# Expert rows of x loaded as 128 pieces of 768 words, and sorted by ScalarE: one layer of a hybrid decoder with a mixture of experts

## The reference

```python
h = rms_norm(x, norm2_g) * (1 + sc2) + sh2          # (T, D)
g_idx   = top-1 of softmax(h @ w_rg + b_rg)         # 4 groups
e_idx   = top-2 of softmax((h @ w_re + b_re) in that group)   # 8 experts each
weights = g_top * e_top / sum(e_top)
for each expert e, over the tokens xs that chose it:
    gate, up = split(xs @ w_e_in[e], 2)             # w_e_in[e]: (1024, 1024)
    y = (silu(gate) * up) @ w_e_out[e]              # w_e_out[e]: (512, 1024)
x = x + gt2 * (sum over both experts of weights * y)
```

## Time and profile before

| | us |
|---|---|
| median of 3 runs | 1781.41 (1779.94 to 1782.64) |
| profiled execution, first to last instruction (span) | 1778.4 |
| median less span | 3.0 |
| TensorE busy | 1670.4 (94%) |
| VectorE busy | 1012.6 (57%) |
| ScalarE busy | 442.4 (25%) |
| DMA traffic | 363.70 MB, mean 205 GB/s |
| chain that ended last | PE 80%, DMA 14%, DVE 3% |

### The profile page before, as it was taken

One profiled execution on the slowest core, in us unless ns is written; L12 is line 12 of the kernel. 1 busy time (PEld: TensorE's weight loads), 2 busy tenths in 40 slices (PEclk: granted clock), 3 DMA queues, 4 the chain that ended last, 5 costly groups with the idle time before them and its releaser, 6 DMA issues.

```text
span 1778.4 us, 35422 instructions
## 1 busy us (share of the span) xinstructions
PE 1670.4 (94%) x14793; PEld 930.9 (52%) x14793; DVE 1012.6 (57%) x2453; ACT 442.4 (25%) x1072; POOL 211.8 (12%) x311
## 2 busy tenths in 40 slices
PE   5999999999999999999999999987999999999990
PEld 3455444544444545555455545545777775555550
DVE  2486526555555354443544435555778877776754
ACT  5120324333444212222122121112222122122110
POOL 3030000000110222202222051010000000000003
PEclk9999999999999999999999999988999999999995
DMA  9377218001211110101101176489899999999997
GB/s 350 120 265 252 71 71 263 25 24 32 63 48 52 47 33 16 33 21 31 34 16 33 56 292 232 148 284 370 330 425 427 426 427 426 429 427 427 429 422 303
DMA packets 109014, 363.70 MB, mean 205 GB/s; under 512 B 12890, under 2 KB 56840, under 8 KB 96428
## 3 DMA queue, kind: packets, MB, share of 16 engines
q1 hardware_dynamic: 86256, 282.70, 41.0%
q10 hardware_dynamic: 15708, 54.73, 8.4%
q0 software_dynamic: 6960, 25.04, 3.8%
HBM read 316.42 MB, written 58.74 MB: 211 GB/s over the span
## 4 chain that ended last, share of the span: by engine, by line
PE 80%; DMA 14%; DVE 3%; POOL 1%; issue 1%; ACT 1%; SPq 1%; ACTq 0%; POOLq 0%; DVEq 0%
PE bank L298 78%; DMA arena<-in_w_e_out 11%; DMA arena<-in_w_in 1%; POOL arena L759 1%; PE bank L945 1%; DMA arena<-y_slots,ints 1%; SPq L380 1%; DVE arena L2396 0%; DVE arena L1887 0%; PE bank L1233 0%; ACTq L1397 0%; DMA arena<-in_kn_g_c 0%; DVE arena L2386 0%; ACT arena L1523 0%; DMA x_slots<-arena,ints 0%
## 5 line engine op out<-in xcount | busy, mean ns | idle before, releaser
L298 PE MATMUL bank<-arena 128*32 128x256 f32 (+7 forms) x14414 | 1627.4, 388 | 36.4 <-DMA arena<-in_w_e_in 7.1
L298 PEld LDWEIGHTS bank<-arena 128*32 128x32 f32 (+3 forms) x14414 | 884.7, 131 | 748.5 <-issue 548.1
L2386 DVE STREAM_TRANSPOSE arena<-arena 32x256 f32<-32x256 f32 x372 | 161.9, 435 | 5.7
L2396 DVE STREAM_TRANSPOSE arena<-arena 32x128 f32<-32x128 f32 x384 | 157.5, 410 | 4.8
L1725 ACT ACTIVATE arena<-bank 128x128 f32<-128x128 f32 x96 | 19.7, 278 | 395.4 <-PE bank L298 395.4
L1717 ACT ACTIVATE arena<-arena 128x96 f32<-128x96 f32 x248 | 92.1, 460 | 5.2 <-DVE arena L2386 5.2
L2377 DVE TENSOR_TENSOR arena<-bank,arena 128x512 f32<-128x512 f32 x64 | 35.5, 557 | 99.9 <-PE bank L298 99.8
L2144 DVE TENSOR_TENSOR arena<-arena,bank 128x128 f32<-128x128 f32 (+1 forms) x40 | 11.4, 286 | 130.3 <-PE bank L298 130.3
L759 POOL DMA_INDIRECT arena<-y_slots,ints x16 | 17.1, 1070 | 542.9 <-DMA y_slots<-arena 537.9
L684 POOL TENSOR_TENSOR arena<-arena 64x256 f32<-64x256 f32 x96 | 70.2, 731 | 30.3 <-DVE arena L2120 23.7
L1887 DVE RECIPROCAL arena<-arena 128x512 f32<-128x512 f32 x10 | 33.5, 3349 | 30.8 <-ACT arena L1452 30.8
(11 more groups left out here) (337 smaller groups left out, 1030.1 us busy)
## 6 DMA issues: line engine op xcount, KB each, us to landing
arena<-in_w_e_in SPq DMA_DIRECT2D x64, 2048.0 KB, 24.4
arena<-in_w_e_out SPq DMA_DIRECT2D x32, 2048.0 KB, 25.2
arena<-in_w_ada SPq DMA_DIRECT2D x12, 2048.0 KB, 12.4
arena<-in_w_in SPq DMA_DIRECT2D x32, 512.0 KB, 3.8
arena<-x_slots ACTq DMA_DIRECT2D x32, 512.0 KB, 10.3
y_slots<-arena ACTq DMA_DIRECT2D x32, 288.0 KB, 9.3
y_slots<-arena POOLq DMA_DIRECT2D x21, 384.0 KB, 17.2
arena<-in_w_in SPq DMA_DIRECT2D x3, 2048.0 KB, 21.3
```

Source lines behind the costliest of these rows:

```text
L298: return nc.tensor.matmul(o, l, r, start=start, stop=stop)
L2386: ins = V.transpose(e_xT[s][ts(b, QT), :, ts(t, QT)], rows[:, :, b, :])
L2396: ins = V.transpose(hT[ts(q, QT), :, ts(t, QT)], e_h[ts(c, QT), r, :].rearrange("p (n k) -> p k n", k=4))
```

## The change

Three things change together.

1. The slot of a token within its expert is no longer its rank r. With third = r // 32 it is 3 (r mod 32) + third: the row 3i + t holds the token of rank 32t + i. `place` computes this with two comparisons, a multiply-add and an addition more.
2. An expert's 96 rows of 1024 words are read as 128 pieces of 768 words in plain order, one per partition. Three rows are four pieces. `turn_x` makes 16 transposes of 32 x 192 of them into a new buffer `e_raw`, of which there is one, so it waits for `e_xT` (the modulation of the expert before) in place of `win_used`.
3. `e_raw` holds the channel tiles out of order: for one channel tile, the 32 tokens of a third are every fourth word. `modulate` reads them so and writes `e_xT[s]` in order. For half of the channel tiles the three thirds lie at one distance and one instruction of 96 columns does it, for the others two are needed (64 and 32 columns).

Expert 0 is still transposed by TensorE; its rows now come by three loads of 32 rows each, every third row, into a buffer of their own (`e_x0`).

```diff
@@ -261,6 +261,7 @@
         r_mem, r_pre = rtmp(2, NE), rtmp(NT, NE)
         x_m = rtmp(NT, TOPK, NE)
         r_slot, r_far = rtmp(TOPK), rtmp(TOPK)
+        r_third = rtmp(2, TOPK)
         r_cnt, r_nx, r_cum, r_ov, r_io = (rtmp(NE) for _ in range(5))
         r_i4, r_iP, r_tok = rtmp(NG), rtmp(P), rtmp(NT)
         r_own, r_over, r_div = (rtmp(NT, TOPK) for _ in range(3))
@@ -279,7 +280,16 @@
 
         WE = [[view(12288 * s + 4096 * j, 4, 1024) for j in range(3)] for s in range(2)]
         WX = [view(32768, 4, 1024), view(24576, 4, 1024), view(28672, 4, 1024)]
-        e_xs = [view(TMP0 + 2322 + D * s, D) for s in range(2)]
+        e_xs = [view(TMP0 + 2322 + 768 * s, D) for s in range(2)]
+        e_x0 = view(36864, D)
+        E_RAW = TMP0 + 2322 + 1536
+        e_raw = view(E_RAW, 6, P)
+
+        def raw_columns(c, k, w, n):
+
+            q = 4 * w + c
+            o = E_RAW + 256 * (q % 3) + P * k + q // 3
+            return SB[:, o:o + 257 * n].rearrange("p (w x) -> p w x", x=257)[:, :, 0:4 * QT - 3:4]
         e_xT = [view(TMP0 + KT * CAP * s, KT, CAP) for s in range(2)]
         e_h, e_hT, e_g = view(36864, 3, P), view(37248, 4, CAP), view(37632, 3, P)
         e_hTl = view(38784, 4, CAP)
@@ -504,7 +514,7 @@
                              .rearrange("a (p k) n -> p (a k) n", p=P)).then_inc(sem("merge_w"), 16)
 
             third(0)
-            sp.wait_ge(sem("xs0_in"), 16)
+            sp.wait_ge(sem("xs0_in"), 48)
             third(1)
             sp.wait_ge(sem("x_used"), 2 * NT)
             for t in range(2):
@@ -1283,9 +1293,9 @@
             pe.wait_ge(sem("router_dve"), COUNTS)
 
 
-            def xT(e, s):
+            def xT(rows):
                 for k in range(KT):
-                    ins = E.transpose(PS[k // 4][:, ts(k % 4, CAP)], e_xs[s][0:CAP, ts(k, P)], ident[0:CAP, 0:CAP])
+                    ins = E.transpose(PS[k // 4][:, ts(k % 4, CAP)], rows[0:CAP, ts(k, P)], ident[0:CAP, 0:CAP])
                 ins.then_inc(sem("xs_used"), 1)
 
 
@@ -1324,8 +1334,8 @@
                 pe.wait_ge(sem("y_out"), 2 * e)
                 second(WE[w], hT)
 
-            pe.wait_ge(sem("xs0_in"), 16)
-            xT(0, 0)
+            pe.wait_ge(sem("xs0_in"), 48)
+            xT(e_x0)
             pe.wait_ge(sem("win00_in"), 16)
             pe.wait_ge(sem("e_xT"), 1)
             first(0, WE[0], 0).then_inc(sem("win_half"), 1)
@@ -1369,7 +1379,7 @@
                         pe.wait_ge(sem("extra_xs"), 16 * j + 16)
                         pe.wait_ge(sem("extra_w"), 48 * j + 48)
                         pe.wait_ge(sem("e_xT"), NE + j)
-                        xT(0, 1)
+                        xT(e_xs[1])
                         pe.wait_ge(sem("e_xT"), NE + j + 1)
                         pe.wait_ge(sem("e_act"), NE + j)
                         first(1, WE[0], 0)
@@ -1696,12 +1706,15 @@
                 A.activation(v, v, ACT.Exp).then_inc(sem("r_exp"), 1)
             act.wait_ge(sem("router_dve"), COUNTS)
 
+            xs_pieces = xslot_d[0:NE * CAP].rearrange("(e a) n -> e (a n)", e=NE).rearrange("e (q n) -> e q n", n=768)
+
             def load_x(e, s):
-                act.dma_start(e_xs[s], xslot_d[ds(CAP * e, P)]).then_inc(sem(f"xs{s}_in"), 16)
+                act.dma_start(e_xs[s][:, 0:768], xs_pieces[ds(e, 1)].rearrange("o q n -> (o q) n")).then_inc(sem(f"xs{s}_in"), 16)
 
             for s in range(2):
                 act.wait_ge(sem(f"x_sc{s}"), 16 * NT)
-            load_x(0, 0)
+            for w in range(3):
+                act.dma_start(e_x0[ts(w, QT)], xslot_d[0:CAP].rearrange("(i t) n -> t i n", t=3)[w]).then_inc(sem("xs0_in"), 16)
             load_x(1, 1)
 
             def xT_out(e, s, ks=KT):
@@ -1714,7 +1727,10 @@
             def modulate(e, s):
                 act.wait_ge(sem("xs_used"), e + 1)
                 for k in range(KT):
-                    ins = A.activation(e_xT[s][:, k, :], e_xT[s][:, k, :], ACT.Identity, scale=sc2e[:, k:k + 1], bias=sh2e[:, k:k + 1])
+                    c = k // 2
+                    for w, n in (((0, 3),), ((0, 2), (2, 1)), ((0, 1), (1, 2)), ((0, 3),))[c]:
+                        ins = A.activation(e_xT[s][:, k, QT * w:QT * (w + n)].rearrange("p (w m) -> p w m", m=QT),
+                                           raw_columns(c, k % 2, w, n), ACT.Identity, scale=sc2e[:, k:k + 1], bias=sh2e[:, k:k + 1])
                 ins.then_inc(sem("e_xT"), 1)
 
             def silu(e, first=False):
@@ -2261,7 +2277,11 @@
                 rank = rank_bank(t).unsqueeze(1).to_broadcast([P, TOPK, NE])
                 link(TT(r_t, r_m[:, t], rank, ALU.mult))
                 link(V.tensor_reduce(out=r_rank[:, t], in_=r_t, axis=AX, op=ALU.add))
-                STT(r_slot, r_v[:, t], -float(CAP), r_rank[:, t], ALU.mult, ALU.add)
+                TS(r_third[:, 0], r_rank[:, t], float(QT), float(1 - 3 * QT), ALU.is_ge, ALU.mult)
+                link(TS(r_third[:, 1], r_rank[:, t], float(2 * QT), float(1 - 3 * QT), ALU.is_ge, ALU.mult))
+                STT(r_slot, r_v[:, t], -float(CAP), r_third[:, 0], ALU.mult, ALU.add)
+                link(STT(r_third[:, 1], r_rank[:, t], 3.0, r_third[:, 1], ALU.mult, ALU.add))
+                link(TT(r_slot, r_slot, r_third[:, 1], ALU.add))
                 link(TS(r_far, r_rank[:, t], float(CAP), float(8 * T), ALU.is_ge, ALU.mult))
                 STT(i_dst[:, TOPK * t:TOPK * t + TOPK], r_slot, float(NE * CAP), r_far, ALU.add, ALU.add)\
                     .then_inc(sem("x_placed"), 1)
@@ -2376,14 +2396,13 @@
                     cols = slice(512 * u, 512 * u + (512, 256)[u])
                     TT(e_y[s][:, cols], PS[5 + u][:, 0:(512, 256)[u]], gt2[:, cols], ALU.mult).then_inc(sem("y_out"), 1)
 
-            def turn_x(e, s, turn, used):
-                dve.wait_ge(sem(f"xs{s}_in"), 16 * turn + 16)
-                if used is not None:
-                    dve.wait_ge(sem("win_used"), used)
-                for t in range(3):
-                    rows = e_xs[s][ts(t, QT), :].rearrange("p (k b n) -> p k b n", b=4, n=QT)
+            def turn_x(e, s, turn):
+                dve.wait_ge(sem(f"xs{s}_in"), 16 * turn + (16 if s else 48))
+                dve.wait_ge(sem("e_xT"), e)
+                for g in range(4):
+                    pieces = e_xs[s][ts(g, QT), 0:768].rearrange("p (k b n) -> p k b n", b=4, n=QT)
                     for b in range(4):
-                        ins = V.transpose(e_xT[s][ts(b, QT), :, ts(t, QT)], rows[:, :, b, :])
+                        ins = V.transpose(e_raw[ts(b, QT), :, ts(g, QT)], pieces[:, :, b, :])
                 ins.then_inc(sem("xs_used"), 1)
 
             def turn_h(e, again=True, hT=e_hT):
@@ -2402,32 +2421,32 @@
             for k in range(4, KT):
                 ins = TS(e_xT[0][:, k, :], PS[1][:, ts(k - 4, CAP)], sc2e[:, k:k + 1], sh2e[:, k:k + 1], ALU.mult, ALU.add)
             ins.then_inc(sem("xT_v"), 1)
-            turn_x(1, 1, 0, None)
+            turn_x(1, 1, 0)
             activate(0, False)
             turn_h(0, False)
-            turn_x(2, 0, 1, 1)
+            turn_x(2, 0, 1)
             activate(1)
             y_out(0, 0, None)
             turn_h(1)
-            turn_x(3, 1, 1, 2)
+            turn_x(3, 1, 1)
             activate(2)
             y_out(1, 1, None)
             turn_h(2)
-            turn_x(4, 0, 2, 3)
+            turn_x(4, 0, 2)
             activate(3)
             y_out(2, 0, 32)
             turn_h(3)
-            turn_x(5, 1, 2, 4)
+            turn_x(5, 1, 2)
             def pair(i):
                 e = 2 * i
                 activate(e)
                 y_out(e - 1, 1, 32 * (i - 1))
                 turn_h(e)
-                turn_x(e + 2, 0, i + 1, e + 1)
+                turn_x(e + 2, 0, i + 1)
                 activate(e + 1)
                 y_out(e, 0, 32 * i)
                 turn_h(e + 1)
-                turn_x(e + 3, 1, i + 1, e + 2)
+                turn_x(e + 3, 1, i + 1)
 
             with dve.Fori(2, 5) as i:
                 pair(i)
```

## The result

| | before | after |
|---|---|---|
| median of 4 runs, us | 1782.03 (1779.94 to 1784.47) | 1795.32 (1792.59 to 1797.68) |
| ratio, 95% interval | | 1.0072 (1.0053 to 1.0091) |
| span of the profiled execution, us | 1778.4 | 1793.6 |
| from the first x tile's transposes to those of expert 0 | 134.78 | 144.84 |
| from SiLU of expert 0 to SiLU of expert 31 | 497.49 | 499.85 |

The change makes the kernel 0.72% slower, about 12.8 us; 1776.9 was forecast. Of the 15.2 us between the two spans, 3.80 lie ahead of the first x tile of the dispatch (1074.07 against 1077.87), where the code is the same: in the profiled executions of all fourteen kernels this point lies anywhere from 1074.07 to 1081.42, so these 3.8 us are spread and no effect of the change.

A forecast was written before the change was run, and what follows sets the result against it. Transfers were taken to bound the late expert stage (16.88 us per expert), TensorE the early part. The new engine chain, just above the transfers, gives -4.85, the last two experts +0.3: together -4.5, so 1776.9 us; range 1774.0 to 1788.

The forecast's parts named there:

- The loads: Full DMA stretch of the expert stage: 25 x loads each get 0.307 us shorter, 7.7 us in all.
- Rival C: Expert-stage loads get no shorter, a 3 KB piece taking as long as a 4 KB row; about 1782.5 us, chance 0.08.
- The start: Tail of `place(7)` (+0.65 us) and expert 0's three loads: expert stage starts 0.5 to 1.4 us late, 0.95 taken.
- VectorE's turn: `turn_x` in the expert stage: 16 transposes of 32x192 at 370 ns take 6.13 us, +0.75 us.
- rival B: Expert stage: the chain of `turn_x` and modulation becomes the whole bound, taking more than loads give; about 1790 us, chance 0.20.
- Twelve instructions in place of eight: ScalarE's modulation per expert: instructions of 96, 64 and 32 columns take 4.09 us, +1.11 us.
- The strided read: ScalarE's modulation reading every fourth word: 0.20 to 0.62 us more per expert, 0.41 us taken.
- Lateness and pace: Steady expert loop: `first(e+2)` ready 0.76 us late in alternate turns, mean 0.38 per expert; TensorE's pace 15.92 us.
- B's own sign: Early part of the expert stage: a pace over 16.1 us per expert would show rival B.
- SiLU of expert 0: ScalarE's modulation of expert 1, ahead of the first SiLU, grows by at most 2.3 us, covered by a 2.63 us wait.
- rival A: Expert stage: transfers stay the bound, reading every fourth word costing 0.20 us or less; 1774.5 us, chance 0.30.

The follow-up runs named there:

- e12: Kernel before with only the x loads of experts 2 to 31 written as 128 pieces of 768 words: 1776.65 us, ratio 0.9966.
- e9: Kernel after with the 2 MB load issued behind the last tile's output matmuls and the 4-byte stores ahead of the dispatch: 1787.83 us, ratio 1.0031.
- e11: Kernel after with the 2 MB load and 4-byte stores moved out of the dispatch and the modulation handed over in halves: 1777.47 us, ratio 0.9972.
- e1: Kernel before with only the four added `place` instructions, their result not used in the slot: 1794.15 us, ratio 1.0060.
- e8: Kernel before with the four added `place` instructions, 4-byte stores ahead of the dispatch, 2 MB load behind the last tile's matmuls: 1783.50 us, ratio 1.0006.
- e4: Kernel after with 2 MB load and 4-byte stores held until tile 4's scatters landed, and ScalarE reading adjacent words: 1787.96 us, ratio 1.0034.
- e10: Kernel after with each expert's modulated columns handed to TensorE in two halves: 1788.25 us, ratio 1.0031.
- e7: Kernel before with the four added `place` instructions and the 2 MB load issued behind the last tile's output matmuls: 1788.54 us, ratio 1.0037.
- e3: Kernel after with only the 4-byte stores held until tile 4's scatters have landed: 1790.90 us, ratio 1.0041.
- e6: Kernel before with the four added `place` instructions and the 4-byte stores issued ahead of the dispatch: 1790.88 us, ratio 1.0044.
- e5: Kernel before with x loads of 96 rows into 96 partitions instead of 128 rows: 1813.77 us, ratio 1.0167.

## Why the prediction was wrong

The forecast was - 4.5 us, the result + 12.8 (9.4 to 16.2), outside the range. Step by step:

- **The loads (right).** 25 x 0.307 = 7.7 us; e12 gave 7.66, and the late pace fell by the 0.31 per expert. Rival C is out.
- **The start (right in size, wrong in place).** The tail of `place(7)` grew by 0.67 and expert 0's loads by 0.13, 0.80 where 0.95 was taken, and D of e9 and e11 is + 1.0. But the step said "`place(6)` grows as much, but under the logits of tile 7", and left every earlier `place` out of the sum, at nothing and without a reason. That is the step that failed first and worst. `place(4)` has no such cover: it sets when a scatter leaves, SyncE's 2 MB load and 4-byte stores leave at a time of their own, and the scatter must be out before tile 6 is written. e1 shows 10.7 us (11.5 in D) from these four instructions alone, and e8 that all but 0.84 of it is gone when that traffic is moved. The row of before, a wait of 1.34 us for the scatter at 1168.34, already showed that this landing had no room left: the prediction moved the instruction, and not the DMA that hangs on it, past its neighbours on the other queues.
- **VectorE's turn (right).** 16 transposes in 6.13 us, 371 ns each. The block price of rival B is out.
- **Twelve instructions in place of eight (right).** e4 has 4.09 us from 1312.21 to 1316.30, as worked out.
- **The strided read (mis-sized).** Taken at 0.41 us per expert, with 0.62 as the upper end; 0.80 measured. 0.54 ns per word was the mean of two VectorE rows (0.26 and 0.81); ScalarE takes 1.03 to 1.05, above both. By the rule cited from the Trainium skill (SBUF — State Buffer, "Door 1: The DMA port swizzle") the price is above nothing, and e4 agrees, with 99 ns on 96 words; the size was a matter for the trace, and no row of this engine was there to give it.
- **Lateness and pace (right in kind).** Two turns in 32.4 us are 31.08 + 1.3, so the lateness is 1.3 us and the mean half of it, 0.65, where 0.76 and 0.38 were forecast. It is shared between the two turns, 0.75 and 0.56, and not the whole in every second one. e4, without the stride, has 0.50 where the sum gives 0.35: the room was 0.15 smaller than I had put it. The rest, 0.39, is the stride. Over 31 turns 0.27 x 31 = 8.4 us separate the forecast from the result, and S came out 7.8 us above the 492 that the forecast implies. It decides the sign: rival B named 1.08 as the point from which the chain eats all that the loads give, and 1.3 is past it. The mean pace of 16.2 is B's own sign, over 16.1. With the dispatch mended (e9) the change still costs 5.5 us in the median, where the forecast had a gain.
- **SiLU of expert 0 (a term too small).** It starts 0.34 later. What stands ahead of it on ScalarE grew by 2.97 us, which is more than the cover of 2.63, where the prediction had "at most 2.3": about 1.9 for the modulation, 0.8 for the turn, and 0.3 because this turn now waits for ScalarE's modulation of expert 0. The prediction had said of that new wait that it "costs nothing", and had looked at the steady loop alone.
- **A slip in rival A.** Its last two experts would take 2 x 15.82 = 31.64 in place of 31.60, so its time is 1774.7 and not 1774.5. Nothing hangs on it.

B was the rival that held in the expert stage, for another reason than the one priced, and at + 2.4 us rather than + 8. It had 0.20. The dispatch, which is four fifths of the loss, was in no rival. Without its loss the time is just inside the range (e9, 1787.83), but still with the wrong sign.

## What to carry to other kernels

When an instruction moves or grows, follow the DMA that it releases as well: compare its issue time with those of the large or fine-grained transfers on the other queues, and ask who waits for its landing. A landing that someone already waits for by a microsecond is a place without cover, however much time the engines around it have. Where a stage stands between transfers and an engine chain with a margin under 2 us, a term that has no row of its own engine should be given a range wider than the rows of another engine allow (here 0.80 us against an upper end of 0.62); and splitting the hand-over in two (e10) is a cheap way to buy the margin.

## What was not expected of the hardware

- VectorE could go on 9.3 us after the issue of an indirect scatter of 128 rows with a 2 MB load 0.92 us behind it and 4-byte stores behind the load, and 17.0 us after it with the load 0.27 us behind. With both moved, the recorded landings are at most 6.8 us after the issue; the second scatter of tile 2, whose landing is not recorded there, is waited for until 8.1 to 8.2 us after it (e8, e9, e11), and so is that of tile 4 in e9 and e11, without delay to TensorE.
- The two kinds of traffic hold such a scatter in different ways: beside the 2 MB load its own packets end later (11.7 to 11.8 us after the issue against 8.8), and with the stores, 2048 packets of 4 bytes, issued 0.3 to 1.1 us behind it, it lands only 3.5 to 5.1 us after its last packet (e7, e10, e1 and the kernel after). In e3 and e6, without them, and before, where they are issued 1.4 us behind it, this takes 0.3 to 0.6 us. Through which queue or order this comes about stays open.
- An x load of 96 rows into 96 partitions lowers the throughput of all 16 DMA engines together from 427 to 391 GB/s, while their busy share stays at 1; 128 pieces of 3 KB with the same bytes don't.
- ScalarE pays 1.03 to 1.05 ns per word for a read of every fourth float32 word, on top of the 0.82 ns per column that the earlier trace rows give for adjacent ones.
- TensorE stood still for 9.2 to 10.6 us ahead of expert 0's transposes in all fourteen kernels, and the mean granted clock over the 13.8 us from the first matmuls on was anywhere from 0.80 (e5, after 9.4 us) to 0.90 (before, e6 and e12, after 9.2 to 9.8 us). The first 192 matmuls took 11.9 to 13.3 us with it, 1.4 us of spread that the length of the wait doesn't explain.
